# Moving the state matrices of samples 3 to 7 behind the routing, and their store into the last expert

## Chip, cores and metric

One core of one Trainium2 chip. The metric is the device time of one execution in microseconds (us); three executions of the kernel before took 1564.03, 1562.56 and 1562.74 us, the median is 1562.74 us.

## What is computed

One inference step of a two-layer decoder for 256 prompt tokens and 8 samples of one token each, 264 tokens of width 1024, all float32. Layer 0 is a pair of gated linear recurrences and a dense feed-forward block. Layer 1 is an mLSTM with 4 heads and a mixture of 8 experts of which each token takes 2. For each sample the mLSTM also returns its new state:

```
def step(carry, inp):                      # L = 1 for a sample
    C, n, m = carry
    ...
    w_c = jnp.exp(b[:, -1] + m - m_new)
    w_s = jnp.exp(b[:, -1:, :] - b + ic - m_new[:, None, :])
    C_new = w_c[..., None, None] * C + jnp.einsum('bsh,bshk,bshv->bhkv', w_s, kc, vc)

def _moe(x, w_router, w1, w3, w2):
    top_v, top_i = lax.top_k((x @ w_router).astype(F32), TOP_K)
    ...
    for e in range(N_EXPERTS):
        y = y + gate[..., e:e + 1] * _swiglu(x, w1[e], w3[e], w2[e]).astype(F32)
```

A sample's C is 4 heads x 128 x 256; the eight of them are 4 MB. Nothing in the rest of the step reads the new C: the sample's output is made from the old C and a correction. C_new only has to be stored.

## The kernel before

Activations lie feature by feature: 8 blocks of 128 features by 264 tokens. Every weight tile (128 x 1024) comes over SP's queue into a ring of four slots (three tiles each in the experts), ScalarE rounds it to the short format (whi, L1858 in the experts, L1383 before), VectorE takes the remainder (wlo, L2632 and L1949), and TensorE makes each product in three matmuls (L597 to L599). whi and wlo have four places: ScalarE rounds tile g+4 when TensorE is done with tile g, VectorE follows ScalarE, TensorE follows VectorE. A ring slot is loaded again when VectorE is done with its last tile.

The order on each engine is written out by hand; an engine does its instructions in that order and waits on semaphores. Around the change it is this.

- *Last output projection of layer 1* (`out_tile(2, k)` on VectorE, L2271, called from L2617 on; `out_projection` on TensorE). The tiles k = 0 to 7 are added to the residual as they come. `base(n, k)` (L2173) takes the sum of the tokens' mean shift out of X for k and k+1 and must have run for k = 6 before TensorE opens the sums of squares and with them its last tile. After k = 5 and k = 6 come sums of residuals and squares (L2209 to L2215, L2193 to L2204).
- *The new matrices* (`new_sample_state(b, first, n)`, L2491). ScalarE has multiplied the old C by w_c in place (L1721). For each head VectorE adds ki times the value row, spread over the partitions (vb1[b]), with one SCALAR_TENSOR_TENSOR on 128 x 256, and waits at the end for its own instructions. Samples 0 to 4 stand in `out_tile`, samples 5 to 7 behind the layernorm.
- *Value rows* (POOL, L2864). POOL spreads the eight rows of 4 KB to 128 partitions into eight places vb1, those of samples 6 and 7 in the gate's region `ogf`, free once the last projection has its input (`xl_ready`).
- *Routing.* TensorE makes the router's logits, turns them (L1202) and turns the tokens in six blocks (L1195); ScalarE copies these to xtok (L1398) and stores them as rows. xtok lies over places of vb1, so ScalarE waits for `cnew_ready` of all samples first. VectorE picks the top two experts, TensorE ranks the tokens (L1213) and fills its waits with spin matmuls (L618); then `gather_first` (L1234) makes the first expert's tokens in two halves, and `split_gathered(0)` (L2719) takes their remainders (L2722).
- *Experts* (`expert(j)` on TensorE L1321, ScalarE L1884, VectorE L2747). An expert has 84 granules g of one weight tile. At g in SILU_AT VectorE makes a SwiGLU product (L2756), at g in TURNED_AT the remainder of the transposed block (L2761), behind ScalarE's copy of it (L1895); at g = 28 it selects the next expert's tokens (L2712 to L2695). Seven experts run in a loop, the last is written out after it and takes in the sums of the others: at g in SUM_ADDED_AT VectorE adds them to R (L2767) and raises `sc_added`, the eighth at g = 71.
- *The store* `o_Cs` (4 MB, POOL, L2866) waits for all eight new matrices and stands ahead of POOL's loop of gathers.

## Time and profile before

| | us |
|---|---|
| median of three executions | 1562.74 (1562.56 to 1564.03) |
| profiled execution, first to last instruction | 1562.3 |
| TensorE busy | 1516.0 (97%) |
| VectorE busy | 1266.8 (81%) |
| ScalarE busy | 1101.9 (71%) |
| GpSimd busy | 39.4 (3%) |
| mean granted TensorE clock | 0.986 of 2.4 GHz |
| HBM read and written | 446.19 MB and 15.89 MB |

The profiled execution's own time is not listed apart from the three, so its span of 1562.3 stands for it. Times in the rows count from the span's start. Experts take the time from 577 to 1538 us. The busy time of TensorE is modelled and says little about idle gaps; gaps are read from the views in order of time, where "[3.44 <-X]" is the idle time before an instruction and what ended it. The granted clock is 1.00 at 2.4 GHz and 0.5 at 1.2 GHz. Queue q1 is SP's, q10 ScalarE's and q0 POOL's.

### The profile page before, as it was taken

To read this page: it belongs to the slowest core of one execution; us is meant where nothing else is said; L and a number is where in the kernel's file an instruction comes from. 1 tells how busy PE (TensorE), PEld (TensorE's weight loads), DVE (VectorE), ACT (ScalarE), POOL (GpSimd) and SP (SyncE) were. 2 spreads that over 40 slices of the span, in tenths; PEclk is the share of its full clock that TensorE was granted. 3 is DMA by queue.
4 is the path that set the end of the run, shared out by engine and by line. 5 is a ranking of instruction groups with operands and counts; after the bars stand their busy time and mean duration, and the time that the engine had idled before them with its cause. 6 is when DMAs were issued, how large, how long until landed. Compare 5 with 4: busy or idle time off the path is not lost.

```text
span 1562.3 us, 24282 instructions
## 1 busy us (share of the span) xinstructions
PE 1516.0 (97%) x8520; PEld 1308.2 (84%) x8520; DVE 1266.8 (81%) x1537; ACT 1101.9 (71%) x1390; POOL 39.4 (3%) x56
## 2 busy tenths in 40 slices
PE   8998999999899899999999999999999999999996
PEld 8888899998788868888888888888888888888884
DVE  5634766666865779999999999999999999999895
ACT  6435644445755658788788788788788788788774
POOL 0000000000001000000000000000000000000000
PEclk9998999999999999999999999999999999999998
DMA  9441655673534449999999999999999999999990
GB/s 359 136 144 56 189 189 190 216 284 108 219 132 176 170 179 357 376 378 383 366 389 382 365 388 382 368 381 377 374 383 376 378 379 378 373 385 371 392 349 36
DMA packets 56340, 461.40 MB, mean 295 GB/s; under 512 B 7185, under 2 KB 7385, under 8 KB 24145
## 3 DMA queue, kind: packets, MB, share of 16 engines
q1 hardware_dynamic: 48672, 424.25, 70.3%
q0 software_dynamic: 5680, 26.91, 5.4%
q10 hardware_dynamic: 1920, 9.35, 1.5%
q8 instruction: 42, 0.69, 0.2%
q14 instruction: 26, 0.21, 0.0%
HBM read 446.19 MB, written 15.89 MB: 296 GB/s over the span
## 4 chain that ended last, share of the span: by engine, by line
PE 81%; issue 9%; DVE 5%; ACT 2%; DMA 1%; SPq 0%; POOL 0%; DVEq 0%; ACTq 0%; POOLq 0%
PE bank L597 24%; PE bank L599 24%; PE bank L598 24%; PE bank L1271 1%; DMA ysum<-yrow,sum_at 1%; DVE state L2496 1%; PE bank L592 1%; DVE wlo L1949 1%; PE bank L746 1%; PE bank L1234 1%; DVE arena L2353 0%; DMA m<-in_m 0%; PE bank L1243 0%; PE bank L743 0%; ACT X L1575 0%
## 5 line engine op out<-in xcount | busy, mean ns | idle before, releaser
L2632 DVE TENSOR_TENSOR wlo<-ring,whi 128x1024 fp32r<-128x1024 f32 x672 | 805.7, 1223 | 68.5 <-ACT whi L1858 30.6
L1858 ACT ACTIVATE whi<-ring 128x1024 fp32r<-128x1024 f32 x672 | 711.7, 1065 | 174.5 <-PE bank L599 165.6
L597 PE MATMUL bank<-whi,high 128*128 128x512 f32 x1344 | 532.5, 396 | 0.6 <-DVE low L2722 0.6
L599 PE MATMUL bank<-whi,low 128*128 128x512 f32 x1344 | 525.1, 391 | 0.0
L598 PE MATMUL bank<-wlo,high 128*128 128x512 f32 x1344 | 524.5, 390 | 0.0
L599 PEld LDWEIGHTS bank<-whi,low 128*128 128x128 f32 x1344 | 252.8, 188 | 53.7
L597 PEld LDWEIGHTS bank<-whi,high 128*128 128x128 f32 x1344 | 252.8, 188 | 52.8 <-DVE wlo L2632 1.4
L598 PEld LDWEIGHTS bank<-wlo,high 128*128 128x128 f32 x1344 | 253.2, 188 | 49.8
L597 PE MATMUL bank<-high,whi 128*128 128x264 f32 x928 | 272.0, 293 | 11.2 <-DVEq L2358 5.9
L598 PE MATMUL bank<-low,whi 128*128 128x264 f32 x928 | 266.5, 287 | 0.0
L599 PE MATMUL bank<-high,wlo 128*128 128x264 f32 x928 | 266.3, 287 | 0.0
L1949 DVE TENSOR_TENSOR wlo<-ring,whi 128x1024 fp32r<-128x1024 f32 x134 | 162.0, 1224 | 110.9 <-ACT whi L1383 105.4
L1383 ACT ACTIVATE whi<-ring 128x1024 fp32r<-128x1024 f32 x134 | 141.6, 1059 | 144.3 <-PE bank L599 135.2
L597 PEld LDWEIGHTS bank<-high,whi 128*128 128x128 f32 x928 | 178.2, 192 | 17.5 <-issue 8.4
L598 PEld LDWEIGHTS bank<-low,whi 128*128 128x128 f32 x928 | 178.3, 192 | 0.2
L599 PEld LDWEIGHTS bank<-high,wlo 128*128 128x128 f32 x928 | 177.5, 191 | 0.0
L1398 ACT ACTIVATE arena<-bank 128x264 f32<-128x264 f32 (+5 forms) x79 | 33.1, 434 | 44.3 <-PE bank L599 36.4
L2304 DVE TENSOR_TENSOR arena<-arena,bank 128x264 f32<-128x264 f32 x22 | 9.5, 430 | 40.0 <-PE bank L599 38.7
L2756 DVE SCALAR_TENSOR_TENSOR arena<-arena,bank 128x512 f32<-128x512 f32 x56 | 41.5, 741 | 0.0
L2761 DVE TENSOR_TENSOR low<-bank,high 128x512 fp32r<-128x512 f32 x56 | 38.2, 683 | 0.0
L1891 ACT ACTIVATE arena<-bank 128x512 f32<-128x512 f32 x56 | 32.6, 582 | 2.3 <-PE bank L599 2.3
L1271 PEld LDWEIGHTS bank<-con,arena 128*128 128x128 f32 x224 | 27.9, 141 | 7.0
(396 smaller groups left out, 1065.9 us busy)
## 6 DMA issues: line engine op xcount, KB each, us to landing
ring<-in_w_moe SPq DMA_DIRECT2D x224, 1536.0 KB, 8.7
ring<-in_w_in SPq DMA_DIRECT2D x24, 1024.0 KB, 5.0
ring<-in_w SPq DMA_DIRECT2D x22, 1024.0 KB, 4.8
ring<-in_w SPq DMA_DIRECT2D x7, 1536.0 KB, 7.5
ring<-in_w_out SPq DMA_DIRECT2D x4, 1536.0 KB, 6.8
state<-in_state ACTq DMA_DIRECT2D x1, 4096.0 KB, 14.7
arena<-vrows POOLq DMA_DIRECT2D x8, 512.0 KB, 5.5
o_Cs<-state POOLq DMA_DIRECT2D x1, 4096.0 KB, 12.4
```

Of the source, the lines that this page charges most:

```text
L597: pe.matmul(out, xh, wh, start=start, stop=False)
L598: pe.matmul(out, xh, wl, start=False, stop=False)
L599: return pe.matmul(out, xl, wh, start=False, stop=stop)
L1271: mm = pe.transpose(bank[TURN_BANK][:, i * P:(i + 1) * P], hb[:, i * P:(i + 1) * P], ident)
L1383: A_(whi[:, g % NSPLIT, :], ring[:, load % RING, part * D:(part + 1) * D], ACT.Copy).then_inc(high_ready, 1)
L1398: return A_(out, see(act, name)[0:rows, 0:n], func, **kw)
L1858: A_(whi[:, g % NSPLIT, :], ring[:, s % RING, (g % 3) * D:(g % 3 + 1) * D], ACT.Copy).then_inc(whi_ready, 1)
L1891: A_(sE, bank[2 * (b % 2)], ACT.Silu).then_inc(silE_ready, 1)
L1949: V.tensor_tensor(wlo[:, g % NSPLIT, :], ring[:, load % RING, part * D:(part + 1) * D], whi[:, g % NSPLIT, :].bitcast(F32), ALU.subtract). ...
L2632: V.tensor_tensor(wlo[:, g % NSPLIT, :], ring[:, s % RING, (g % 3) * D:(g % 3 + 1) * D], whi[:, g % NSPLIT, :].bitcast(F32), ALU.subtract) ...
L2756: V.scalar_tensor_tensor(out=hb, in0=sE, scalar=slot[:, 1:2], in1=bank[2 * (b % 2) + 1], op0=ALU.mult, op1=ALU.mult).then_inc(hb_ready, 1)
L2761: V.tensor_tensor(hTl[:, b % 2].rearrange("p f n -> p (f n)"), bank[TURN_BANK], hTh[:, b % 2].bitcast(F32).rearrange("p f n -> p (f n)"), ...
```

## The change

VectorE makes samples 0 to 2 where it did. Samples 3 and 4 are made between the two halves of the first gather, samples 5, 6 and 7 in the first expert after granules 13, 25 and 37. The first expert is therefore written out ahead of the loop, which begins at 1. ScalarE's wait ahead of the token copies is for three samples, and it waits for all eight ahead of an expert's output copy. The value rows of samples 6 and 7 get other places (`arg`, `t1`, `nsb`), behind waits that POOL meets earlier. The store `o_Cs` moves on POOL from ahead of the loop of gathers to behind it and waits for `sc_added` of all eight sums.

```diff
--- before.py
+++ after.py
@@ -83,6 +83,7 @@
 SUM_BANK, SUM_AT = 7, [2, 3, 4, 5]
 SUM_ADDED_AT = {(W13_AT[_b + 1] if _i else W2_AT[_b - 1]) + NSPLIT - 1: 2 * _n + _i for _n, _b in enumerate(SUM_AT) for _i in range(2)}
 SELECT_AT, PICK_AT = 28, 56
+STATES_AT = {13: 5, 25: 6, 37: 7}
 AHEAD = 8
 ARENA = 23376
 STATE = 8256
@@ -264,8 +265,9 @@
         Pr = region(2 * 384).rearrange("p (a n) -> p a n", a=2)
         kw = region(2 * 256).rearrange("p (a s n) -> p a s n", a=2, s=2)
         DK_AT = cur[0] - 2 * (384 + 384 + 256)
+        ARG_AT = cur[0]
         vb1 = [qkf[:, 0:D], qkf[:, D:2 * D], vtokf[:, 0:D], vtokf[:, D:2 * D], arena[:, DK_AT:DK_AT + D],
-               arena[:, DK_AT + D:DK_AT + 2 * D], ogf[:, 0:D], ogf[:, D:2 * D]]
+               arena[:, DK_AT + D:DK_AT + 2 * D], arena[:, ARG_AT:ARG_AT + D], arena[:, ARG_AT + D:ARG_AT + 2 * D]]
         arg = region(2 * 256).rearrange("p (a n) -> p a n", a=2)
         t1 = region(2 * NP_).rearrange("p (a n) -> p a n", a=2)
         nsb = region(2 * 512).rearrange("p (a n) -> p a n", a=2)
@@ -1861,7 +1863,7 @@
             act.wait_ge(lgT_ready, 1)
             act.nop().then_inc(freed("lgT"), 1)
             wait_layer1_stored(act)
-            act.wait_ge(cnew_ready, NS)
+            act.wait_ge(cnew_ready, 3)
             for t, (t0, n) in enumerate(TT):
                 for a in range(2):
                     take(("xt", t, a), xtok[0:n, t, a * 512:(a + 1) * 512], ACT.Copy, n=512, rows=n).then_inc(xtok_ready, 1)
@@ -1900,6 +1902,7 @@
                 y = yh if last else yrow
                 act.wait_ge(y_psum, j + 1)
                 if not last:
+                    act.wait_ge(cnew_ready, NS)
                     act.wait_ge(y_added, j * 16 + 16)
                 A_(y[:, 0:BLK], bank[4], ACT.Copy).then_inc(yh_ready, 1)
                 act.wait_ge(granule_used, j * GPJ + (GPJ + NSPLIT))
@@ -2617,12 +2620,10 @@
             tile(23)
             for k in range(NSPLIT):
                 out_tile(2, k, g=TOUT1 + NSPLIT + k, state=(k // 2, 2 * (k % 2), 2))
-            for k in range(NSPLIT, KD - 1):
-                out_tile(2, k, state=(k - 2, 0, MH))
-            out_tile(2, 7)
+            out_tile(2, NSPLIT, state=(2, 0, MH))
+            for k in range(NSPLIT + 1, KD):
+                out_tile(2, k)
             layernorm(2)
-            for b in range(5, NS):
-                new_sample_state(b, 0, MH)
             dve.wait_ge(x_ready, KD * 3)
 
             def rest_of_granule(j, g):
@@ -2716,8 +2717,11 @@
                 V.scalar_tensor_tensor(out=sum_at[:], in0=free_row[:, 1:2], scalar=float(N), in1=slot[:, 0:1],
                                        op0=ALU.add, op1=ALU.add).then_inc(sum_at_ready, 1)
 
-            def split_gathered(j):
+            def split_gathered(j, between=()):
                 for a in range(2):
+                    if a == 1:
+                        for b in between:
+                            new_sample_state(b, 0, MH)
                     dve.wait_ge(xgh_ready, j * 2 + (a + 1))
                     V.tensor_tensor(xgl[:, 4 * a:4 * a + 4, :].rearrange("p k n -> p (k n)"), bank[GATHER_BANK[a]],
                                     xgh[:, 4 * a:4 * a + 4, :].bitcast(F32).rearrange("p k n -> p (k n)"),
@@ -2731,7 +2735,7 @@
             V.tensor_copy(nmore[:], mcnt[0:1, 3:4]).then_inc(more_ready, 1)
             for g in range(NSPLIT):
                 rest_of_granule(0, g)
-            split_gathered(0)
+            split_gathered(0, between=(3, 4))
             row_numbers(0, FIRST_SLOT_BANK)
             own.settle(V.tensor_scalar(R[:], X[:], ALPHA, None, ALU.mult))
             for g in range(NSPLIT, AHEAD):
@@ -2744,12 +2748,14 @@
                 cols = slice(a * BLK, (a + 1) * BLK)
                 V.tensor_tensor(yl[:, cols], bank[4 + a], yh[:, cols].bitcast(F32), ALU.subtract).then_inc(yl_ready, 1)
 
-            def expert(j, last=False):
+            def expert(j, last=False, states={}):
                 slots(j)
                 if last:
                     V.tensor_scalar(GT[:], tokens[:], slot[:, 0:1], None, ALU.is_equal).then_inc(gt_ready, 1)
                 for g in range(AHEAD, GPJ):
                     rest_of_granule(j, g)
+                    if g in states:
+                        new_sample_state(states[g], 0, MH)
                     if g in SILU_AT:
                         b = SILU_AT[g]
                         dve.wait_ge(silE_ready, j * NBLK + (b + 1))
@@ -2787,7 +2793,8 @@
                     dve.wait_ge(sc_psum, KD + k + 1)
                     V.tensor_tensor(R[:, k, :], R[:, k, :], bank[SCATTER_BANK[k]][:, 0:N], ALU.add).then_inc(r_ready, 1)
 
-            with dve.Fori(0, more * NE + (NE - 1)) as j:
+            expert(0, states=STATES_AT)
+            with dve.Fori(1, more * NE + (NE - 1)) as j:
                 expert(j)
             expert(more * NE + (NE - 1), last=True)
             dve.wait_ge(r_ready, 4 * KD)
@@ -2860,10 +2867,9 @@
                 if b == 6:
                     pool.wait_ge(cout_ready, MH)
                     pool.dma_start(A["o_Cp"][:, MH - 1], Cout[:, (MH - 1) % 2, :]).then_inc(cp_stored[MH - 1], 16)
-                    pool.wait_ge(xl_ready, 5 * KD)
+                if b == 7:
+                    pool.wait_ge(psum_ready, J[("tns", MH - 1)] + 1)
                 pool.dma_start(vb1[b], bc(vrows[b:b + 1], [P, D])).then_inc(vb1_loaded[b], 16)
-            pool.wait_ge(cnew_ready, NS)
-            pool.dma_start(A["o_Cs"], state[:, 0:8192]).then_inc(stored, 16)
 
             def fetch_rows():
 
@@ -2887,6 +2893,9 @@
                 pool.wait_ge(y_added, j * 16 + 16)
             pool.dma_start(xtok[:, 0:2, :], ysum[0:2 * P].rearrange("(t p) n -> p t n", t=2)).then_inc(y_added, 16)
             pool.dma_start(xtok[0:NS, 2, :], ysum[2 * P:N]).then_inc(y_added, 16)
+            pool.wait_ge(cnew_ready, NS)
+            pool.wait_ge(sc_added, KD)
+            pool.dma_start(A["o_Cs"], state[:, 0:8192]).then_inc(stored, 16)
             pool.wait_ge(out_ready, 1)
             pool.dma_start(A["o_y"], X[:]).then_inc(stored, 16)
             pool.wait_ge(stored0, 32)
```

The order of instructions moves in three places. The first is VectorE in the last output projection, from the group of sample 2 on (L2496, in the change L2499); L2173 (L2176) is base(6). Before:

```order
L2496 SCALAR_TENSOR_TENSOR state<-arena,state 128x256 x4
L2180 TENSOR_TENSOR R<-R,bank 128x264
L2496 SCALAR_TENSOR_TENSOR state<-arena,state 128x256 x4
L2209 TENSOR_TENSOR SQ<-R 128x528
L2210 TENSOR_TENSOR SQ<-SQ 128x264
L2173 SCALAR_TENSOR_TENSOR R<-X,bank 128x528
L2180 TENSOR_TENSOR R<-R,bank 128x264
L2496 SCALAR_TENSOR_TENSOR state<-arena,state 128x256 x4
L2215 TENSOR_TENSOR SQ<-SQ,R 128x264
```

With the change:

```order
L2499 SCALAR_TENSOR_TENSOR state<-arena,state 128x256 x4
L2183 TENSOR_TENSOR R<-R,bank 128x264
L2212 TENSOR_TENSOR SQ<-R 128x528
L2213 TENSOR_TENSOR SQ<-SQ 128x264
L2176 SCALAR_TENSOR_TENSOR R<-X,bank 128x528
L2183 TENSOR_TENSOR R<-R,bank 128x264
L2218 TENSOR_TENSOR SQ<-SQ,R 128x264
```

The groups of samples 3 and 4 are gone ahead of base(6) and of the last sums.

The second is VectorE from the first granules on, `low<-bank,high` being the halves of the gathered tokens; then, in the first expert, from the SwiGLU product at g = 11 to granule 28. Before, the gather:

```order
L2632 TENSOR_TENSOR wlo<-ring,whi 128x1024 x4
L2722 TENSOR_TENSOR low<-bank,high 128x512 x2
L2701 COPY arena<-bank 128x2
L2702 TENSOR_SCALAR row_at<-bank 128x1
L2736 TENSOR_SCALAR R<-X 128x2112
L2632 TENSOR_TENSOR wlo<-ring,whi 128x1024 x4
```

With the change, the gather:

```order
L2633 TENSOR_TENSOR wlo<-ring,whi 128x1024 x4
L2726 TENSOR_TENSOR low<-bank,high 128x512
L2499 SCALAR_TENSOR_TENSOR state<-arena,state 128x256 x8
L2726 TENSOR_TENSOR low<-bank,high 128x512
L2702 COPY arena<-bank 128x2
L2703 TENSOR_SCALAR row_at<-bank 128x1
L2740 TENSOR_SCALAR R<-X 128x2112
L2633 TENSOR_TENSOR wlo<-ring,whi 128x1024 x4
```

and the first expert:

```order
L2762 SCALAR_TENSOR_TENSOR arena<-arena,bank 128x512
L2633 TENSOR_TENSOR wlo<-ring,whi 128x1024 x2
L2499 SCALAR_TENSOR_TENSOR state<-arena,state 128x256 x4
L2633 TENSOR_TENSOR wlo<-ring,whi 128x1024 x2
L2767 TENSOR_TENSOR low<-bank,high 128x512
L2633 TENSOR_TENSOR wlo<-ring,whi 128x1024 x4
L2762 SCALAR_TENSOR_TENSOR arena<-arena,bank 128x512
L2633 TENSOR_TENSOR wlo<-ring,whi 128x1024 x6
L2499 SCALAR_TENSOR_TENSOR state<-arena,state 128x256 x4
L2633 TENSOR_TENSOR wlo<-ring,whi 128x1024 x2
L2767 TENSOR_TENSOR low<-bank,high 128x512
L2633 TENSOR_TENSOR wlo<-ring,whi 128x1024
```

The two halves stand apart with eight instructions between them, and a group of four follows granule 13 and granule 25; the third follows granule 37. The remainders and products keep their order.

The third is POOL. Before, the store is issued ahead of the loop:

```order
L2862 DMA o_Cp<-arena 128x257
L2864 DMA arena<-vrows 128x1024 x2
L2866 DMA o_Cs<-state 128x8192
L2876 TENSOR_LOAD nmore
L2876 ISA x2
```

With the change it follows the loop's end and the load of the sums:

```order
L2883 COMPARE_AND_BRANCH
L2894 DMA arena<-ysum 128x2x1024
L2895 DMA arena<-ysum 8x1024
L2898 DMA o_Cs<-state 128x8192
L2900 DMA o_y<-X 128x2112
```

It stands between the loads of the sums and the store of the output.

## Rows read from the trace of the kernel before

**Rows 1.** The page's chain that ended last: shares of the span by line.
```profile
PE bank L597 24%; PE bank L599 24%; PE bank L598 24%; PE bank L1271 1%; DMA ysum<-yrow,sum_at 1%; DVE state L2496 1%; PE bank L592 1%; DVE wlo L1949 1%; PE bank L746 1%; PE bank L1234 1%; DVE arena L2353 0%; DMA m<-in_m 0%; PE bank L1243 0%; PE bank L743 0%; ACT X L1575 0%
```

**Rows 2.** ScalarE in time, two roundings; columns: start us, us, engine, line, operation, count [idle before <-releaser].
```profile
615.54 1.07 ACT L1858 ACTIVATE whi<-ring 128x1024 fp32r<-128x1024 f32 x1 [0.32 <-PE bank L599]
...
616.90 1.06 ACT L1858 ACTIVATE whi<-ring 128x1024 fp32r<-128x1024 f32 x1 [0.29 <-PE bank L599]
```

**Rows 3.** VectorE in time, the last output projection.
```profile
535.90 1.67 DVE L2496 SCALAR_TENSOR_TENSOR state<-arena,state 128x256 f32<-128x256 f32 x4 [0.21 <-DVE R L2180]
...
538.93 0.70 DVE L2173 SCALAR_TENSOR_TENSOR R<-X,bank 128x528 f32<-128x528 f32 x1
...
545.15 0.42 DVE L2180 TENSOR_TENSOR R<-R,bank 128x264 f32<-128x264 f32 x1
```

**Rows 4.** TensorE in time, first matmul of the projection's last tile.
```profile
539.84 0.36 PE L597 MATMUL bank<-high,whi 128*128 128x264 f32 x1 [3.44 <-issue]
```

**Rows 5.** Stretches: us, busy (count) of PE, PEld, DVE, ACT, POOL, granted PE clock, DMA share, GB/s.
```profile
513.00:517.00 4.00, 2.32 (x18) 2.14 (x18) 3.82 (x12) 2.37 (x7) 0.00 (x0) 1.00 0.17 71
...
536.00:540.00 4.00, 0.56 (x5) 0.38 (x4) 3.75 (x8) 1.76 (x5) 0.00 (x0) 1.00 0.06 27
540.00:544.00 4.00, 4.00 (x21) 3.90 (x20) 3.24 (x8) 0.42 (x1) 0.00 (x0) 0.57 0.01 2
577.20:581.00 3.80, 3.71 (x10) 2.93 (x11) 1.48 (x5) 1.06 (x1) 0.00 (x0) 0.60 0.02 6
```

**Rows 6.** VectorE in time, ahead of the routing.
```profile
557.06 1.68 DVE L2496 SCALAR_TENSOR_TENSOR state<-arena,state 128x256 f32<-128x256 f32 x4 [0.21 <-DVE state L2496]
...
559.53 0.18 DVE L2642 COPY arena<-bank 128x16 f32<-128x16 f32 x1
```

**Rows 7.** TensorE in time, the routing.
```profile
556.13 0.31 PE L1202 MATMUL bank<-con,SQ 8*128 8x8 f32 x3
...
560.88 0.99 PE L618 MATMUL bank<-high 128*128 128x264 f32 x6 [1.32 <-DVE arena L2651]
...
563.91 3.50 PE L618 MATMUL bank<-high 128*128 128x264 f32 x16
```

**Rows 8.** VectorE in time, first granules and gather.
```profile
567.31 4.61 DVE L2632 TENSOR_TENSOR wlo<-ring,whi 128x1024 fp32r<-128x1024 f32 x4
...
576.55 0.69 DVE L2722 TENSOR_TENSOR low<-bank,high 128x512 fp32r<-128x512 f32 x1 [3.53 <-ACT high L1881]
```

**Rows 9.** VectorE in time, first expert, after the selection.
```profile
618.08 3.50 DVE L2632 TENSOR_TENSOR wlo<-ring,whi 128x1024 fp32r<-128x1024 f32 x3 [0.23 <-ACT whi L1858]
```

**Rows 10.** TensorE in time, first expert, granule 29.
```profile
619.42 0.43 PE L597 MATMUL bank<-whi,high 128*128 128x512 f32 x1
```

**Rows 11.** VectorE in time, last expert, the eighth turned sum.
```profile
1516.72 0.42 DVE L2767 TENSOR_TENSOR R<-R,bank 128x264 f32<-128x264 f32 x1
```

**Rows 12.** DMA issues: operands, queue, count, KB, us to landing.
```profile
o_Cs<-state POOLq DMA_DIRECT2D x1, 4096.0 KB, 12.4
```

**Rows 13.** DMA queues, 1518.3 to 1530: packets, MB, share of 16 engines.
```profile
q1 hardware_dynamic: 187, 1.90, 45.1%
```

**Rows 14.** DMA queues, 564 to 570.
```profile
q0 software_dynamic: 67, 2.20, 85.3%
q10 hardware_dynamic: 64, 0.26, 10.6%
```

**Rows 15.** DMA queues, 1431 to 1447.
```profile
q1 hardware_dynamic: 520, 5.69, 84.8%
q0 software_dynamic: 304, 1.08, 16.7%
```

**Rows 16.** ScalarE in time, last expert, granule 81.
```profile
1529.17 1.07 ACT L1858 ACTIVATE whi<-ring 128x1024 fp32r<-128x1024 f32 x1 [0.22 <-PE bank L599]
```

**Rows 17.** TensorE in time, last expert, first matmul of granule 80.
```profile
1532.26 0.49 PE L597 MATMUL bank<-whi,high 128*128 128x512 f32 x1
```

**Rows 18.** Stretch 800 to 900, columns as in rows 5.
```profile
800.00:900.00 100.00, 100.00 (x459) 82.85 (x458) 93.15 (x95) 82.51 (x88) 2.68 (x2) 1.00 0.95 373
```


## The prediction

> **What bounds the kernel now.** I read the page's chain first: 72% of it are the matmuls of the expert and projection loops [rows 1], so TensorE sets the end and a gain has to be a gap of TensorE. All eight experts run that way; a granule (one tile of 128 x 1024 weights, six matmuls) takes TensorE 1.36 us, the distance of two ScalarE roundings that each wait for it [rows 2]. Then I read VectorE and TensorE in time where the diff touches them: the last output projection (535 to 546 us), the routing (556 to 577), the first expert at the granules named in STATES_AT, and the end of the last expert. Between layer 1 and the experts it is VectorE that is waited for, and eight groups of four SCALAR_TENSOR_TENSOR (1.67 us, 1.89 with the wait for their own end) stand there in its order.
>
> The profiled execution spans 1562.3 us. The sum below is made against it; the median of the three times, 1562.74, lies 0.44 above, and I add that. About 0.2% (3.1 us) is what a measurement of this kernel can tell from no change.
>
> **A: samples 3 and 4 leave the last projection, -3.6 us.** Sample 3 stands between the fifth residual and the sum that precedes base(6), which starts at 538.93 [rows 3]; sample 4 follows one residual later in the same way. TensorE's last tile needs base(6) and was idle 3.44 us for it [rows 4]. Without the 1.89 us, base(6) starts at 537.04, the tile at 537.95. The rest of VectorE's chain down to the last residual (545.15) loses sample 4 too, 3.8 us together, and would be ready at 541.4. The tile itself took from 539.84 to about 545.0, just ahead of that residual, because the granted clock stood at 0.57 in the four microseconds after that idle time [rows 5]; 24 matmuls and a sum at full clock are 3.4 us (a granule's matmul takes 0.227 for 512 columns, so one of 264 takes 0.12). The remaining gap is 1.6 us. In 513:517, where TensorE was busy 2.3 of 4 us, the clock stayed at 1.00 [rows 5], so I take full clock: tile done 541.4, last residual 541.6, all that follows 3.6 us earlier. With the low clock the tile ends near 543.2 and A is -1.8. These are the bounds.
>
> **B: samples 5 to 7 leave the place ahead of the routing, -1.9 us together with what takes their place.** The three groups end at 558.7, and the first copy of the router's logits follows at 559.53 [rows 6], although TensorE had them turned at 556.44 [rows 7]. So VectorE's part starts 3.0 us sooner, and ScalarE, which waited for all eight matrices, is free as well. Not all of it arrives: TensorE's idle 1.32 us ahead of its six spin matmuls goes, then those spins are late next, so the ranks are computed 1.6 us earlier, not 3.0. VectorE then splits four granules (ends at 570.3 instead of 571.92), and halves of the gathered tokens. Between these halves now stand samples 3 and 4. Before, VectorE was idle there for 3.53 us [rows 8], up to 576.55; two groups need 3.77. TensorE's gather set the second half, and sixteen spins at 3.50 us held that gather [rows 7]. Now VectorE sets it: 570.3 plus 0.69 for the first half plus 3.77 gives 574.7, 1.9 sooner. If spins or gather run at low clock for longer, I get 1.4; with the gather the bound at full clock, 3.1. ScalarE's, SP's and POOL's other steps only move with this. The earlier loads of samples 6 and 7 (two of 512 KB) compete only with expert weights that are wanted 60 us later: nothing.
>
> **C: three groups inside the first expert, +2.1 us.** Four granules are in flight: ScalarE rounds g+4 when g is used, VectorE subtracts (1.22 us, 1.14 in a row). Ready is 2.35 us after TensorE is done with g, wanted 4.08 us after, so the slack is 1.7. A group of 1.89 uses it up; afterwards VectorE regains some 0.2 per granule (1.36 against 1.14), less what the SwiGLU products and transposed remainders take. At g = 13 and g = 37 that leaves 0.2 to 0.3 of idle TensorE each. At g = 25 it is worse: three granules later stands the selection for the next expert, and VectorE's split of g = 29, begun at 618.08, ends at 619.30, while TensorE starts on it at 619.42 [rows 9, 10]. There the slack is zero, so what is left of the group (1.89 less about 0.5) is all stall: 1.4. Stalled time is not regained, since TensorE is the bound. Sum 2.1; bounds 0.6 (only the excess over one slack at each place) and 5.65 (all three groups exposed).
>
> **D: the 4 MB store in the last expert, +5.0 us.** Before, it ran from 559 to 571 with an empty DMA behind it; now POOL issues it when VectorE adds the eighth turned sum, at 1517.2 of the old time [rows 11]. From issue to landing it took 12.4 us [rows 12]; its packets alone need 9.8 (below) and ScalarE's between them 1.5, so data begins about 1.1 us after the issue, at 1518.3. The ring still has 187 packets to come then (some 33 of them tiny), 154 of 12 KB, or 9.7 on each of 16 engines [rows 13]. How two queues share is in [rows 14]: while this store ran against ScalarE's rows, 67 of its packets went with 64 of theirs, although one is 32 KB and the other 4 KB. They alternate by packet, not by byte. A store packet took 1.22 us of an engine (85.3% of 16 engines in 6 us over 67), a ring packet 0.47 (84.8% of 16 engines in 16 us over 463 large ones) [rows 15]. Eight rounds of 1.69 and 1.7 packets more are 14.3 us: the last slot lands at 1532.6. ScalarE wants it for g = 81 at 1529.17, and there it had waited for TensorE, not for a load [rows 16]. It is 3.4 us late. This passes whole to TensorE, because ScalarE copies the last transposed block only after g = 81, and g = 80 already needs it: TensorE starts g = 80 at 1532.26, with a matmul of 0.49 instead of 0.39, so already at the limit [rows 17]. After such a gap the clock falls as after the 3.44 us one: 3.8 us at 0.60 held 10 matmuls where 16.7 of 0.227 fit [rows 5], which I round to 1.6 us. 3.4 and 1.6 are 5.0. Bounds: 0, if the ring keeps its rate, and 5.5.
>
> The rest of the store (done by about 1533) lies under the final layernorm; o_y, behind it on POOL, is issued at the very end and is not held up.
>
> A page speaks of POOL's side. The Trainium skill, SBUF — State Buffer, section SBUF: two separate sides, says that VectorE in certain two-port modes locks GpSimd out, so that it can't write the descriptors of its DMAs. By it the store would begin late under a VectorE that is nearly always busy here, and D would be near 0. The one row that bears on it, POOL's 1 MB load at 1431 to 1447, shows 304 POOL packets moved beside 520 of the ring [rows 15], which neither shows nor excludes a late start.
>
> **Sum:** -3.6 - 1.9 + 2.1 + 5.0 = +1.6; span 1563.9, time 1564.3.
>
> **Rivals.** (1) *The store does not disturb the ring*, chance 0.22. It starts late because POOL is slow to get its descriptors out beside a busy VectorE, or the ring's queued packets go ahead. A start 4 us later leaves four ring packets per engine, which land by 1529.2, and D is 0: span 1558.9, time 1559.3. For it: in 1431 to 1447 the ring kept 5.69 MB against POOL's 1.08. Against: there POOL's packets were 4 KB. (2) *The clock stays low in the last projection tile*, chance 0.12: A is -1.8, time 1566.1, slower. It decides if 1.6 us of idle time is enough to lower the clock, as 3.44 was; 513:517 speaks against it. (3) *The groups in the first expert are wholly exposed*, chance 0.07: VectorE is 93% busy in the experts [rows 18], and if each group meets a full queue ahead of it TensorE loses 5.65 instead of 2.1, time 1567.9, slower by more than 0.2%. It decides from about 3.7 us of idle TensorE in that expert on. (4) *The change gives VectorE nothing*, because the routing hangs on ScalarE's token copies: A stays, B is 0, 1566.2, chance 0.03. The forecast has 0.56, within 1562.3 to 1566.2.
>
> **Numbers.** Likeliest 1564.3. Rival 1 sits at the lower end; 1559.0 to 1566.4 takes in it, the forecast and rival 2. Faster by over 0.2% (below 1559.6): two thirds of rival 1 and a little for a cheaper C, 0.20. Slower by over 0.2% (above 1565.9): rivals 2 to 4 and the forecast's upper tail, 0.22. Within 0.2%: 0.58.
>
> **What would show it.** A: the gap ahead of the last out tile is 1.6 us and its matmuls are 0.12 apart. B: VectorE is the releaser of the first expert matmul, 5.5 us earlier than 577.29. C: idle TensorE in the first expert 2.1 us, mostly at g = 29. D: ScalarE waits 3.4 us for a ring DMA at g = 81 and the granted clock dips in the last slices. The prediction is wrong if that wait is absent, if the clock dips near 538, or if VectorE is not what the first expert matmul waits for.

## The result: 0.3% slower, and the profile after

Eight runs of each kernel on the same chip gave a median of **1567.95 us** for the changed kernel (1563.96 to 1570.06) and of **1563.07 us** for the kernel before (1559.3 to 1564.04). The ratio is 1.0028, 95% interval 1.0017 to 1.0040: slower by about 4.4 us. The prediction, 1564.3 with a range up to 1566.4, had the sign and a third of the size; the measured median lies outside its range. Of all executions reported below, one, of the kernel with the store behind the loads, took 1882 us at a mean granted clock of 0.75; it is left out.

The profiled execution of the changed kernel is the longest of its eight: span 1568.2, time 1570.06. Three of the eight took 1564.0 to 1564.6 us, and only the longest was profiled, so the terms below are those of this execution. It reached the last output projection 1.3 us later than the kernel before did, in a part that the edit does not touch. So times are compared below from one point on: **T0**, the moment at which TensorE ends the last but one tile of that projection (start of the last tile's first matmul, less the idle time printed behind it). From there the program is cut in four stretches:

| us | T0 to row numbers | first expert | to last expert's output | end |
|---|---|---|---|---|
| before | 40.82 | 117.33 | 844.17 | 23.6 |
| changed | 35.03 | 119.00 | 852.62 | 23.9 |
| difference | **-5.79** | **+1.67** | **+8.45** | +0.3 |

The first ends with the start of `row_at` (L2703, before L2702), the second with the last split of gathered tokens (L2726, before L2722), the third with the first matmul of L1304 (L1302) that takes the last expert's output back to tokens. The differences add up to +4.6 us, close to the difference of the medians (4.9).

**The last output projection (A).** TensorE in time, changed kernel: the first matmuls of the last tile. They answer to [rows 4].

```profile
539.22 0.36 PE L599 MATMUL bank<-high,whi 128*128 128x264 f32 x1 [1.55 <-issue]
539.41 0.28 PE L600 MATMUL bank<-low,whi 128*128 128x264 f32 x1
539.53 0.28 PE L601 MATMUL bank<-high,wlo 128*128 128x264 f32 x1
```

Idle 1.55 us instead of 3.44, and the matmuls stand 0.12 apart: full clock. The stretch views say the same (us, busy and count of PE, PEld, DVE, ACT, POOL, granted PE clock, DMA share, GB/s; the first row answers to 540:544 in [rows 5], the second to 577.2:581):

```profile
539.20:543.20 4.00, 3.98 (x28) 3.56 (x28) 3.19 (x7) 0.42 (x1) 0.00 (x0) 1.00 0.00 0
...
572.80:576.80 4.00, 4.00 (x11) 3.18 (x12) 1.84 (x3) 1.06 (x1) 0.00 (x0) 0.61 0.00 0
```

**Ahead of the first expert (B).** VectorE in time, changed kernel:

```profile
554.27 0.17 DVE L2643 COPY arena<-bank 128x16 f32<-128x16 f32 x1 [1.72 <-PE bank L1204]
...
563.20 4.61 DVE L2633 TENSOR_TENSOR wlo<-ring,whi 128x1024 fp32r<-128x1024 f32 x4
567.74 0.67 DVE L2726 TENSOR_TENSOR low<-bank,high 128x512 fp32r<-128x512 f32 x1
568.34 1.65 DVE L2499 SCALAR_TENSOR_TENSOR state<-arena,state 128x256 f32<-128x256 f32 x4
570.21 1.67 DVE L2499 SCALAR_TENSOR_TENSOR state<-arena,state 128x256 f32<-128x256 f32 x4 [0.22 <-DVE state L2499]
572.03 0.69 DVE L2726 TENSOR_TENSOR low<-bank,high 128x512 fp32r<-128x512 f32 x1
```

The copy of the logits starts 5.3 us earlier than in [rows 6], the four granules end 4.1 us earlier than in [rows 8]; counted from T0, these are 6.5 and 5.4 us. The idle 3.53 us ahead of the second half of the gather [rows 8] is gone: samples 3 and 4 fill it, and VectorE releases TensorE. TensorE in time, first matmul of the first expert, which stood at 577.29 before:

```profile
572.78 0.50 PE L599 MATMUL bank<-whi,high 128*128 128x512 f32 x1 [1.62 <-DVE low L2726]
```

**In the first expert (C).** TensorE in time at granule 29, which answers to [rows 10]:

```profile
615.05 0.39 PE L600 MATMUL bank<-wlo,high 128*128 128x512 f32 x1
615.28 0.39 PE L601 MATMUL bank<-whi,low 128*128 128x512 f32 x1
616.41 0.50 PE L599 MATMUL bank<-whi,high 128*128 128x512 f32 x1 [0.74 <-DVE wlo L2633]
```

Matmuls in a row start 0.23 apart, these two 1.13: 0.90 lost here, behind the group at g = 25. Granule 29 starts 43.63 us after the first expert matmul, before it was 42.13 [rows 10]; so 0.6 was lost ahead of it (0.45 of this in three steps just behind the group at g = 13), and 0.2 is lost behind it. Behind the group at g = 37 TensorE shows no gap that the kernel before does not have.

**In the last expert (D).** Here the loss lies. ScalarE in time, changed kernel; the row of 1533.28 answers to [rows 16]:

```profile
1524.14 2.01 ACT L1860 ACTIVATE whi<-ring 128x1024 fp32r<-128x1024 f32 x2
1533.28 1.06 ACT L1860 ACTIVATE whi<-ring 128x1024 fp32r<-128x1024 f32 x1 [7.13 <-DMA ring<-in_w_moe]
1534.25 0.58 ACT L1897 ACTIVATE high<-bank 128x512 fp32r<-128x512 f32 x1
```

TensorE in time, granule 80, answering to [rows 17]:

```profile
1536.33 0.79 PE L599 MATMUL bank<-whi,high 128*128 128x512 f32 x1 [6.81 <-DVE low L2767]
1536.92 0.63 PE L600 MATMUL bank<-wlo,high 128*128 128x512 f32 x1
1537.34 0.63 PE L601 MATMUL bank<-whi,low 128*128 128x512 f32 x1
1537.77 0.63 PE L599 MATMUL bank<-whi,high 128*128 128x512 f32 x1
```

ScalarE is ready for g = 81 at 1526.15 (without the load's delay TensorE would have held it until about 1526.4) and waits 7.13 us for the last weight load. TensorE stands for 6.81 us, and then its matmuls are 0.43 apart, half clock, until 1539.5: another 1.6. Together that is the 8.45 of the table.

DMA issues of the changed kernel, 1510 to 1536 (operands, queue, count, KB each, us from issue to landing; [rows 12] had 12.4):

```profile
o_Cs<-state POOLq DMA_DIRECT2D x1, 4096.0 KB, 18.3
```

Its DMA queues in the 4.2 us from the store's first packet on, then in the next 4.5 and the next 4.5 (packets, MB, share of 16 engines):

```profile
q0 software_dynamic: 45, 1.47, 81.5%
q1 hardware_dynamic: 42, 0.50, 28.1%
```
```profile
q0 software_dynamic: 55, 1.80, 92.9%
q1 hardware_dynamic: 27, 0.18, 9.7%
```
```profile
q0 software_dynamic: 44, 0.92, 47.4%
q1 hardware_dynamic: 6, 0.04, 2.0%
```

First 45 store packets go with 42 ring packets, then there are ever fewer ring packets: most engines have moved their part of the last load. But six are left until the end, three of them of 12 KB, and a load has landed only when all its packets have. In the list of packets of the trace the last ring packets of 12 KB start at 1519.52, 1521.19, 1522.86, 1524.52, 1526.19, 1527.85, 1529.52 and 1531.19: eight packets, 1.67 us apart, which is 0.46 of a ring packet and 1.21 of a store packet. The list doesn't name the engines, but a packet starts within 0.01 us of the end of another, so it can be joined into sixteen chains. From the store's first packet of an engine on, ring and store take strict turns in every chain. The chains had between two and eight ring packets of 12 KB left, the one in work at 1519.83 included; the one with eight, all of the last load, is the one above, and it closes last, at 1532.85. The mean engine had 3.6 that had not begun (58 packets on 16 engines). The Trainium skill, DMA: Bandwidth & Descriptors, section Why a DMA increments its semaphore by 16 and not by 1, says that the engines finish independently and that only the full count means that all data has landed; the trace agrees, with 9.3 us between the first (1523.56) and the last (1532.85) of the load's sixteen closing packets, against 2.0 in the kernel before.

The second thing that these packets show: the store's first one starts at 1519.83, 4.8 us after POOL issued it at 1515.04, where I had counted on 1.1; the sixteen engines begin with it between 4.8 and 6.3 us after the issue.

### The profile page after: what moved, and what is told of

Same layout as the page of the kernel before. It is cut to its first block, busy times and chain, and to the rows that moved or that the text cites. A ratio compares the mean times of both kernels' runs of the same rounds, so it can differ in the third digit from the quotient of the medians.

```text
span 1568.2 us, 24190 instructions
## 1 busy us (share of the span) xinstructions
PE 1516.0 (97%) x8520; PEld 1305.0 (83%) x8520; DVE 1266.1 (81%) x1537; ACT 1102.6 (70%) x1390; POOL 40.6 (3%) x56
## 4 chain that ended last, share of the span: by engine, by line
PE 86%; DVE 6%; issue 5%; ACT 2%; DMA 0%; SPq 0%; ACTq 0%; DVEq 0%; POOL 0%; POOLq 0%
PE bank L599 26%; PE bank L600 25%; PE bank L601 25%; DVE wlo L2633 2%; PE bank L1273 1%; PE bank L594 1%; PE bank L748 1%; DVE wlo L1952 1%; DVE arena L2356 0%; DMA m<-in_m 0%; DVE state L2499 0%; ACT X L1577 0%; PE bank L1245 0%; PE bank L745 0%; ACT high L1576 0%
```

## Experiments

Theory 1: the loss is the last weight load, held up by 32 KB rows that alternate with its own packets on the engine that is furthest behind. The rivals are that the loss has its cause before the last expert (Theory 2), and that the store's bytes, not its packets, hold the load up (1b). "Packet" is a row as the trace records it.

### The store behind everything, and its terms by themselves

**Late store.** The store waits until VectorE has split the first half of the last expert's output.

```diff
             pool.wait_ge(cnew_ready, NS)
-            pool.wait_ge(sc_added, KD)
+            pool.wait_ge(yl_ready, 1)
             pool.dma_start(A["o_Cs"], state[:, 0:8192]).then_inc(stored, 16)
```

> The changed kernel, with the 4 MB store of the new matrices issued only when VectorE has split the first half of the last expert's output (about 1540 us) instead of at its eighth turned sum (1515.0). By then every weight load has landed. Theory 1 (the store holds up the last weight load): the terms read from the changed kernel's trace are -3.5 in the last projection, -2.3 at the routing, +1.7 in the first expert, and all that is left of its loss comes from the store. Without it: 1563.1 - 4.1 = 1559.0 us; ScalarE waits for no load at g = 81 and the granted clock stays full up to the final layernorm. Theory 2 (the loss has its cause before the last expert, in the groups or in a different phase of the clock upstream): the store's place does not matter, 1567 to 1568. Theory 3 (a store this late holds up the end itself): it needs 12 to 18 us from 1540 on, so landed by 1558, before o_y is issued at about 1555 to 1561; if it were exposed, o_y would be late and the time above 1565.

Measured: 1559.22 us median against 1562.15 of the kernel before, ratio 0.9976 (0.9964 to 0.9988). Third stretch 844.36, the 844.17 of before within 0.2; no load is waited for. Theory 2 and Theory 3 fall: D comes from the store's place. What is left of the change, from T0 on, is -3.9 us.

**Only the store.** The kernel before, with nothing changed but the store's place.

```diff
-            pool.wait_ge(cnew_ready, NS)
-            pool.dma_start(A["o_Cs"], state[:, 0:8192]).then_inc(stored, 16)
...
+            pool.wait_ge(sc_added, KD)
+            pool.dma_start(A["o_Cs"], state[:, 0:8192]).then_inc(stored, 16)
             pool.wait_ge(out_ready, 1)
```

> The kernel before, with nothing changed but the place of the 4 MB store: behind the eighth turned sum of the last expert, as in the changed kernel. It prices that term by itself. By my prediction (the mean engine has 9.7 ring packets to alternate with, data 1.1 us after the issue): 3.4 of waiting and 1.6 of low clock, 1563.1 + 5.0 = 1568. By theory 1 as the changed kernel's trace shows it (data 4.6 us after the issue, and the engine furthest behind decides): the store is issued at 1517.2, moves from 1521.8, the last load, which landed at 1525.2 before, lands up to eight rounds of 1.67 us later, at 1532 to 1535, wanted at 1529.2: 3 to 6 us of waiting and 1.6 to 3 of low clock, 1568 to 1572. By theory 2 (the loss lies elsewhere): 1563.

Measured: 1570.85, ratio 1.0054 (1.0035 to 1.0072), which is +8.4 us. ScalarE in time at g = 81, and TensorE at granule 80:

```profile
1539.35 1.06 ACT L1858 ACTIVATE whi<-ring 128x1024 fp32r<-128x1024 f32 x1 [7.40 <-DMA ring<-in_w_moe]
```
```profile
1542.40 0.79 PE L597 MATMUL bank<-whi,high 128*128 128x512 f32 x1 [7.16 <-DVE low L2761]
```

Issued at 1520.47, first packet at 1525.16 (4.7 us), landed 13.8 us later: third stretch 853.04, +8.9. So the term is nearly the same without the rest of the change, and my 5.0 for it is refuted in isolation too. Here the last engine still had ten ring packets, and eight store rows went between them; more cannot, because the store has just eight rows (128 on 16 engines) for each engine. (The profiled run's first stretch is longer, 46.5, because its granted clock stayed at half for 20 us from about 563 on; I have no reason for that.)

### Packets or bytes

**Small packets.** Same place, same bytes, rows of 4 KB.

```diff
-            pool.dma_start(A["o_Cs"], state[:, 0:8192]).then_inc(stored, 16)
+            for i in range(8):
+                c = slice(i * 1024, (i + 1) * 1024)
+                pool.dma_start(A["o_Cs"][:, c], state[:, c]).then_inc(stored, 16)
```

> The changed kernel, same place of the store, same bytes, but issued as eight DMAs of 1024 columns each, so that a row is a packet of 4 KB (0.16 us of a DMA engine in the trace before) instead of 32 KB (1.21 us). Theory 1a (packets of the two queues alternate one for one, and a load lands when the last of the 16 engines has moved its eight packets): from the first store packet on, the last load needs at most 8 x (0.46 + 0.16) = 5.0 us instead of 8 x (0.46 + 1.21) = 13.4, lands at about 1525, 1.3 us before ScalarE wants it, and the time is that of the late store, 1559 to 1560. Theory 1b (the store's bytes come first, or the engines are simply full: 4.2 MB at 343 GB/s are 12.2 us, whatever the packets): the load lands at about 1532 as now, and the time stays at 1566 to 1568.

Measured: 1556.15, ratio 0.9969 (0.9957 to 0.9981), and in a second series (below) 0.9965. 1b falls. DMA queues from the store's first packet (1514.12, 4.0 us after the issue) to the load's landing at 1519.04:

```profile
q0 software_dynamic: 307, 1.16, 56.5%
q1 hardware_dynamic: 86, 0.86, 40.7%
```

The load lands 4.9 us after the store's first packet, and eight times 0.46 + 0.16 are 5.0. That agreement is in part chance: the engine that closed last moved its first store row only at 1516.4, and from there its ring packets stand 0.62 apart. ScalarE waits for no load. The eight DMAs were issued over 5 us, so the store also came bit by bit; 272 of its 1024 rows had started when the load landed.

**Half rows.** Two DMAs of 4096 columns, rows of 16 KB.

```diff
-            pool.dma_start(A["o_Cs"], state[:, 0:8192]).then_inc(stored, 16)
+            for i in range(2):
+                c = slice(i * 4096, (i + 1) * 4096)
+                pool.dma_start(A["o_Cs"][:, c], state[:, c]).then_inc(stored, 16)
```

> The changed kernel, same place of the store, as two DMAs of 4096 columns, so that a packet is 16 KB. Rows of 32 KB took 13.0 us from the first store packet to the last load's landing (eight rounds of 0.46 + 1.21 are 13.4), rows of 4 KB 4.9 us (eight of 0.46 + 0.16 are 5.0). By theory 1a a row of 16 KB (about 0.61 us of an engine, halved from 1.21) gives 8 x 1.07 = 8.6 us: with the store's data from 4 to 4.8 us after the issue at 1515 the load lands at 1527.5 to 1528.5, against 1526.3 when ScalarE wants it, a wait of 1 to 2 us; TensorE idles as long, and 0.5 to 1 more for the clock: 1559 + 2 = 1560.5 to 1562. By theory 1b (it is the packets' number that counts, or a threshold between 4 and 32 KB): all of the wait of 7 (1567) or none of it (1557 to 1559).

Measured: 1559.66, ratio 0.9980 (0.9959 to 1.0), with single runs from 1557.7 to 1565.1. In the profiled execution (1558.75) the last ring packets are 1.06 or 1.07 us apart, as 0.46 + 0.61 are, but the last engine began only six of them from the store's first packet on: landed after 5.8 us, at 1522.67, 0.6 before ScalarE wanted it. The size of a round is as expected, the number of rounds was not eight. How far the last engine lags differs from one execution to the next, and a median of ten runs leaves open how often the load is late; the four runs above 1562 would fit such cases, but they were not profiled.

**Behind the loads.** SP issues the store on the ring's own queue, behind its last load.

```diff
                     with sp.Fori(0, NE) as e:
                         expert(p * NE + e, e * FE)
+            sp.wait_ge(cnew_ready, NS)
+            sp.dma_start(A["o_Cs"], state[:, 0:8192]).then_inc(cs_stored, 16)
```

> The changed kernel, with the store issued by SP behind its last weight load, on the ring's own queue, instead of by POOL. Theory 1 (two queues alternate by packet): packets of one queue go in order, so the store's 32 KB rows start only when the engine has moved its part of the last load, the load lands at about 1523, and the time is 1559.0 as with the late store. Rival (any store of this size beside the last loads delays them, or rows of 32 KB block the queue): the wait of 7 us stays, 1566 to 1568. Beside it the row of the first store packet tells whether data also begins 4.6 us after the issue where POOL does not write the descriptors.

Measured: 1558.74 (median of eleven), ratio 0.9978 (0.9968 to 0.9987); third stretch 844.36. One queue keeps its order: no engine moves a ring packet after its first store row. 32 KB rows as such do no harm. The store's packets carry the ring's queue number but differ in size: the first of 32 KB starts at 1517.11, 4.3 us after SP issued it at 1512.81. So a store that POOL does not issue begins late here too, but this one stands behind the last load in its own queue, so it says little about POOL's.

### Why the data began 4.8 us late

**Beside a busy VectorE.** The late store, issued when VectorE has split granule 78 of the last expert, with the last load landed.

```diff
                     rest_of_granule(j, g)
+                    if last and g == 78:
+                        dve.nop().then_inc(tail_at, 1)
```

> The late store, but issued when VectorE has split granule 78 of the last expert (about 1524): the last weight load has landed, so the DMA engines are empty, while VectorE works without a gap until 1530.6. In the changed kernel the store's first packet came 4.8 us after its issue, with full DMA engines and a busy VectorE; with both free (the late store) it came 1.15 us after it. Theory V (VectorE keeps POOL from writing the descriptors): first packet again 4 to 5 us after the issue, or when VectorE pauses. Theory Q (the ring's packets, already in the engines' queues, go first): 1.2 us. The time is that of the late store by both, 1558 to 1560.

Measured: 1559.29, ratio 0.9976 (0.9962 to 0.9990). POOL in time, and the stretch views around its issue:

```profile
1520.88 0.58 POOL L2901 DMA_DIRECT2D o_Cs<-state  x1 [93.83 <-DVEq L2759]
```
```profile
1521.00:1522.00 1.00, 1.00 (x6) 0.83 (x5) 1.00 (x3) 1.00 (x3) 0.46 (x1) 1.00 0.00 0
1521.00:1525.00 4.00, 4.00 (x22) 3.31 (x21) 4.00 (x5) 3.51 (x6) 0.46 (x1) 1.00 0.92 393
```

VectorE is busy for all of these 4 us, and the first packet starts at 1522.03, 1.15 us after the issue, just as in the late store. There I had taken VectorE to be free, which it was not; it was adding the last sums when POOL issued the store at 1535.33:

```profile
1535.30 1.11 DVE L2794 TENSOR_TENSOR R<-R,bank 128x264 f32<-128x264 f32 x3
```

In the kernel before, the store's data began 1.11 us after the issue with VectorE busy for 0.81 of them. So Theory V falls for a busy VectorE by itself. The Trainium skill, SBUF — State Buffer, section SBUF: two separate sides, tells of a VectorE that locks POOL out in two-port modes; these rows show no such thing beside a granule split and a SwiGLU product.

With a full ring the start took 4.0 to 5.0 us in all seven profiled executions of that kind, with an empty one 1.1 to 1.15 in five. That fits Theory Q, but not as I put it: in the changed kernel 58 ring packets, of a load that SP had issued 0.9 us before the store, started behind the store's first packet, so the queued packets do not all go first. Nothing was run with a full ring and an idle VectorE, nor with another amount queued. What makes the start late beside a full ring stays open.

### The other terms

**Samples 3 and 4 back in the projection**, on top of the late store.

```diff
-            act.wait_ge(cnew_ready, 3)
+            act.wait_ge(cnew_ready, 5)
...
-            out_tile(2, NSPLIT, state=(2, 0, MH))
-            for k in range(NSPLIT + 1, KD):
-                out_tile(2, k)
+            for k in range(NSPLIT, KD - 1):
+                out_tile(2, k, state=(k - 2, 0, MH))
+            out_tile(2, 7)
...
-            split_gathered(0, between=(3, 4))
+            split_gathered(0)
```

> The late store, but with samples 3 and 4 back in the last output projection, as in the kernel before, and nothing between the halves of the first gather. It takes the first term of the change (-3.5) away and lets the second grow: VectorE does not hold the second half of the gather any more, TensorE with its sixteen spins does, which I bounded at 3.1 instead of 1.9 (2.3 in the trace). So against the late store +3.5 and -0.8 to -1.2: 1559.2 + 2.5 = 1561.7 (before x 0.9995 to 1.0005). The gap ahead of the last out tile is 3.4 us again, its clock low after it, and the first expert's first matmul waits for VectorE's split with 0 to 1 us. Rival (the two groups cost the same wherever they stand on VectorE's chain): 1559.2, no difference.

Measured: 1560.56, ratio 0.9989 (0.9976 to 1.0001). First stretch 38.33 instead of 35.05: +3.3, where I expected +2.3 to +2.7. TensorE in time, last tile and first expert matmul; then the stretches behind T0:

```profile
536.33 0.56 PE L599 MATMUL bank<-high,whi 128*128 128x264 f32 x1 [3.44 <-issue]
...
571.29 0.50 PE L599 MATMUL bank<-whi,high 128*128 128x512 f32 x1 [0.57 <-DVE low L2726]
```
```profile
534.00:538.00 4.00, 1.67 (x7) 1.70 (x8) 3.54 (x9) 0.67 (x2) 0.00 (x0) 0.62 0.00 0
536.30:540.30 4.00, 3.97 (x18) 4.00 (x19) 3.25 (x8) 0.42 (x1) 0.00 (x0) 0.50 0.01 2
538.00:542.00 4.00, 4.00 (x18) 3.79 (x18) 3.09 (x7) 0.00 (x0) 0.00 (x0) 0.52 0.01 2
```

The 3.44 us gap is back, and the clock falls after it, here for 6.8 us in the trace's list of clock levels where the kernel before had 3.4. So the gap costs more than its own length, and what a low clock adds to it varies.

**No groups in the first expert**, on top of the late store. The kernel leaves out the new matrices of samples 5 to 7.

```diff
-STATES_AT = {13: 5, 25: 6, 37: 7}
+STATES_AT = {}
```

> The late store without the three groups in the first expert: the new matrices of samples 5 to 7 are left out and stored as they came. It prices the third term by itself. By the trace of the changed kernel the first expert took 1.66 us longer (115.76 instead of 114.10 from its first matmul to the last split), so 1559.2 - 1.7 = 1557.5. Rival (most of it is regained later, because VectorE and ScalarE run ahead of TensorE again): 1559.0. Rival (the groups also delay the selection and with it later experts): 1556 or less.

Measured: 1556.69, ratio 0.9962 (0.9949 to 0.9974). First expert 117.24 instead of 118.69, third stretch 844.37 in place of 844.36: the groups cost 1.5 to 1.7 us there (1.7 against the other kernels with the same three groups, 118.93 to 119.00), nothing of it is regained and nothing is lost later. By the ratios the times differ by 2.2 us, more than that, but within what they resolve.

**Groups in twelve pieces**, with small packets, and **all five samples in twenty pieces**, with nothing between the halves of the first gather.

```diff
-STATES_AT = {13: 5, 25: 6, 37: 7}
+STATES_AT = {_g: (5 + _n // 4, _n % 4, 1) for _n, _g in enumerate([10, 13, 16, 19, 22, 33, 36, 39, 42, 45, 48, 51])}
...
-                        new_sample_state(states[g], 0, MH)
+                        new_sample_state(*states[g])
```

> The small-packet store, and the three groups of the first expert cut into their twelve instructions of 0.42 us, one behind every third granule (g = 10 to 22 and 33 to 51), away from the selection at g = 28. Theory (TensorE loses only what exceeds the slack of 1.7 us, and VectorE regains 0.2 us a granule): a piece of 0.42 to 0.6 is regained before the next, the first expert takes 117.3 to 117.6 us from the first row numbers to the last split, as in the kernel before and without groups, instead of 119.0, and the time is 1.4 to 1.6 below the small-packet kernel. Rival (each microsecond of VectorE in the first expert costs TensorE the same share, 1.6 for 5.0 us, wherever it stands): 119.0 as now, and the time of the small-packet kernel.

> As spread_groups, but samples 3 and 4 go into the first expert too, twenty pieces in all, and nothing stands between the halves of the first gather. With samples 3 and 4 back in the projection the stretch from its last tile to the first expert was only 0.2 us shorter than the first term explains, so the gather is by then held by TensorE with its spins: 0.2 us to gain there and no more. If twenty pieces still fit into the slack: 0 to 0.3 below spread_groups. If they don't (20 x 0.42 is 8.4 us, and VectorE regains 0.2 in each of 76 granules, 15 us, less the fourteen products and splits of 0.7 in between, 9.8): 1 to 3 us above it.

> The small-packet kernel once more, beside spread_groups on the same chip, so that their difference can be read: its ratio to the kernel before was 0.9969 with 7 runs; the same, 0.996 to 0.998, is expected.

Measured, against 1563.05 of the kernel before:

| kernel | median us | ratio (95%) | T0 to row numbers | first expert |
|---|---|---|---|---|
| small packets again | 1556.64 | 0.9965 (0.9950 to 0.9981) | 35.03 | 118.98 |
| twelve pieces | 1557.44 | 0.9964 (0.9951 to 0.9977) | 35.05 | 117.57 |
| twenty pieces | 1556.33 | 0.9957 (0.9945 to 0.9969) | 34.00 | 119.25 |

Twelve pieces bring the first expert to 117.57, 0.2 from the kernel before: nearly all of their cost is gone. The pieces are smaller and also stand away from the selection at g = 28; which of the two does how much was not varied. Twenty pieces don't fit. TensorE in time, all five samples spread:

```profile
594.84 0.50 PE L599 MATMUL bank<-whi,high 128*128 128x512 f32 x1 [0.23 <-DVE wlo L2633]
...
600.83 0.50 PE L599 MATMUL bank<-whi,high 128*128 128x512 f32 x1 [0.26 <-DVE wlo L2633]
...
614.44 0.50 PE L599 MATMUL bank<-whi,high 128*128 128x512 f32 x1 [0.57 <-DVE wlo L2633]
```

Against the twelve they gain 1.1 ahead of the expert (I expected 0.2) and lose 1.7 in it, 0.6 us over both (I expected 1 to 3). Over both stretches that is 1.4 us less than small packets for the twelve and 0.8 less for the twenty. The trace resolves this; the medians don't, as five to seven runs scatter over 3 to 5. All three beat both kernels of the case, by 0.35 to 0.43% the one before.

## Why the prediction was wrong

**A, -3.6: right.** The gap is 1.55 (predicted 1.6), the clock 1.00, and the last residual stands 3.5 us earlier against T0 than before. Rival 2 is out. Of the three signs that were to show the prediction wrong, none came: the wait for a load is there, the clock does not dip near 538, and VectorE releases the first expert matmul.

**B, -1.9: right, slightly low.** First stretch -5.79, less A's 3.5, is -2.3; VectorE is the releaser, as forecast, and the first expert starts 5.8 us earlier against T0 where 5.5 was the sum of A and B. The copy of the logits comes 3.0 sooner (6.5 less A's 3.5), as forecast; the four granules end 1.9 sooner instead of 1.6, and the first half with the two groups takes 4.3 us instead of 4.46. Rival 4 is out.

**C, +2.1: right in kind, 0.4 too large.** Measured 1.67, most of it at granule 29 and none regained, but 0.9 there instead of 1.4: VectorE had more in hand at g = 25 than the 0.5 I took. Behind g = 13 it was up to 0.6 instead of 0.2 to 0.3, behind g = 37 nothing that shows as a gap. Rival 3 is out.

**D, +5.0: right in mechanism, wrong in size, and this is the miss.** Measured 8.45 (8.9 with the store alone), 3.45 more; B and C gave 0.8 of it back. The wait for the load at g = 81 is 7.1 instead of 3.4; the price of the low clock, 1.6, was right. Two steps of the 3.4 failed, in opposite directions:

- *"so data begins about 1.1 us after the issue"*. It begins after 4.8. That price came from a store with empty DMA engines. By itself this error would have made the term smaller: with 58 ring packets left, 3.6 for the mean engine, 3.6 rounds of 1.67 end at 1525.8, ahead of the 1526.15 at which ScalarE wants the load. That is rival 1: its condition, a start 4 us later, came true, and its D = 0 did not.
- *"9.7 on each of 16 engines"*. I divided the packets that were left by sixteen. A load is done when its last engine is, and in the profiled run the last one had all eight packets of the last load before it: 8 x 1.67 = 13.4 us from 1519.52, when the first of the eight began, to 1532.85; from the store's first packet that is 13.0. The trace of the kernel before could have said that engines drift: the closing packets of its last load are spread over 2.0 us, or four ring packets of 0.46, with nothing else on the engines.

The sum itself shows how luck hid the second error. Predicted were 1.1 to the first packet and 14.3 to the landing, less 12.0 from the issue to the moment at which ScalarE wants the load: 3.4. Measured are 4.8 and 13.0, less 11.3 (POOL issued the store 0.7 us after the eighth sum, which I had left out), and 0.4 from the landing to ScalarE: 6.9, close to the 6.81 for which TensorE stood. So the 3.5 us in between are the late start (+3.7), the 0.7 and the 0.4, less 1.3. The 14.3 came near to 13.0 because too many rounds were counted from too early a start for the mean engine, while the last one really had eight from the later start.

The alternation itself, the 1.67 us of a round and its place in ScalarE's and TensorE's chain were as predicted; the rounds of 0.62, 1.07 and 1.67 us for 4, 16 and 32 KB rows show it three times. The Trainium skill, DMA: Bandwidth & Descriptors, section Queues, rings and completion order, says that an engine drains a packet of some 9 to 17 descriptors from a queue before it switches. Here the records alternate one row for one row. If a row were one descriptor, a load's eight rows would have gone in one turn, which these traces don't show; how many descriptors a row of 12 or 32 KB has, they don't tell.

My range ended at 1566.4, just above rival 2, with D bounded at 5.5, for which the prediction gives no working. A bound for the wait should have put the start and the engine at their worst together: begun 4 to 5 us late, with all eight packets of the last load still to go on one engine.

## What to carry to other kernels

A large store beside loads that are waited for costs them by its row size: each of their packets waits for one of its rows, on the slowest of the engines, so count the packets of one load per engine times (own packet + store packet), from the store's first packet on, not a mean over all that is left. The store's rows per engine are the cap: here eight of 1.21 us, 9.7 us. Issue such a store behind the last load, on the loads' own queue, or cut its rows; each turned this change from 0.3% slower to 0.2 to 0.35% faster. Work that is moved under another engine's bound costs what exceeds the slack at its place: three groups of 1.9 us cost 1.7, twelve pieces of a quarter of one, placed away from the selection, cost 0.2.

## What the runs showed of the hardware

- A DMA that POOL issued while the ring was full moved its first byte 4.0 to 5.0 us after the issue, one with idle DMA engines 1.15 us after it, with VectorE fully busy. Not all that was queued went ahead of it: 58 ring packets issued earlier started later.
- Sixteen engines that share each load evenly, by eight packets, still drifted apart: with 32 KB rows between, the closing packets of one load were spread over 9.3 us, against 2.0. In the kernel before, the four last loads closed over 2.0 to 3.3 us, in the changed kernel the last but one over 3.9, before the store had moved a row. Why one engine falls behind is open.
- The four profiled executions whose store went in eight DMAs of 4 KB rows had a last stretch of 22.6 to 23.0 us, all others 23.5 to 24.1. I have no cause for that.
- Up to 5 us of difference between profiled executions lies ahead of T0 (532.7 to 537.7), in a part of the program that is nearly the same in all of them. From a common point the third stretch agrees within 0.4 us (844.17 to 844.55) in all kernels in which no load was late, where medians of six to twelve runs resolve 2.
